# A three-stage tail between attention and gathered rows: two halves of two tiles in place of one tile and three

## What is computed

```
ox_att = _attend_blocks(qx, cat(kx, kc), cat(vx, vc))       # 8 heads, 768 keys
mix_x = _merge(gates, hgrn, conv, ox_att @ w_att_o, w_out)  # (...) @ w_out
x = _layer_norm_2(ALPHA * x + xg1 * mix_x, ln1_g, ln1_b)
t = _modulate(x, xsh2, xsc2)
# _peer(t):
q = (t @ wq).reshape(128, 8, 2, 128)
s1, s2 = q[:, :, 0] @ k1.T, q[:, :, 1] @ k2.T
v1, i1 = lax.top_k(s1, 16); v2, i2 = lax.top_k(s2, 16)
score, ci = lax.top_k(v1[..., :, None] + v2[..., None, :], 16)
expert = i1[ci // 16] * 128 + i2[ci % 16]
g = softmax(score)
act = gelu(einsum('thkd,td->thk', u_tab[expert], t))
out = einsum('thk,thkd->td', g * act, v_tab[expert])
x = _layer_norm_2(ALPHA * x + xg2 * out, ln2_g, ln2_b)
```

## Time and profile before

| | us |
|---|---|
| median of three runs | 4299.42 (4298.96, 4299.42, 4314.07) |
| the profiled execution, its own time | 4277.35 |
| its span in the trace | 4275.5 |
| first indirect load issued | 2539.6 |
| last indirect load issued | 4243.6 |

### The profile page before, as it was taken

How to read it: one execution, slowest core, us unless ns; L and a number is a source line. 1 busy time by engine, 2 the same in 40 slices (tenths; PEclk the granted TensorE clock), 3 DMA queues, 4 the chain that set the end, 5 groups by cost and what they waited for, 6 DMA issues and landing times.

```text
span 4275.5 us, 33127 instructions
## 1 busy us (share of the span) xinstructions
PE 3543.1 (83%) x10814; PEld 1818.0 (43%) x10814; DVE 2175.2 (51%) x4744; ACT 910.9 (21%) x1890; POOL 1332.9 (31%) x1241
## 2 busy tenths in 40 slices
PE   8368998999998989979999974768676878776877
PEld 4244544444454565546544564334232323232323
DVE  0567524421004466756525448864687876433443
ACT  1224412000023124622111312111121212111111
POOL 0200000000000005600001013453777777777775
PEclk9667999999999999979899987889988998899999
DMA  3010021343221212211212356774999999999997
GB/s 149 13 50 1 1 99 66 141 158 136 80 79 47 82 59 74 89 54 60 89 59 79 130 188 217 254 254 173 384 344 351 349 370 364 360 371 372 357 373 284
DMA packets 171914, 765.17 MB, mean 179 GB/s; under 512 B 19256, under 2 KB 19256, under 8 KB 160224
## 3 DMA queue, kind: packets, MB, share of 16 engines
q0 software_dynamic: 157904, 580.06, 36.9%
q1 hardware_dynamic: 13824, 182.97, 11.4%
q10 hardware_dynamic: 16, 0.02, 0.0%
HBM read 744.08 MB, written 18.89 MB: 178 GB/s over the span
## 4 chain that ended last, share of the span: by engine, by line
PE 51%; DVE 15%; issue 9%; POOL 6%; DMA 4%; ACT 3%; another core or an unknown queue 1%; POOLq 0%; DVEq 0%; ACTq 0%
PE ps L252 14%; PE ps L258 12%; POOL arena L2742 6%; PE ps L1406 6%; DVE arena L2772 5%; PE ps L1336 5%; PE ps L2695 5%; DMA arena<-in_pu,arena 3%; PE ps L1712 2%; PE ps L220 2%; DMA arena<-in_pv,arena 1%; PE ps L1699 1%; PE ps L786 1%; PE ps L2320 1%
## 5 line engine op out<-in xcount | busy, mean ns | idle before, releaser
L2695 PE MATMUL ps<-arena 128*128 128x512 f32 x2048 | 1024.1, 649 | 369.7 <-issue 158.6
L2772 DVE CUSTOM_DVE_ANT_0 arena<-arena 128x1024 f32<-128x1024 f32 x512 | 623.5, 1222 | 406.7 <-DMA arena<-in_pu,arena 374.1
L2695 PEld LDWEIGHTS ps<-arena 128*128 128x128 f32 x2048 | 400.3, 205 | 974.2 <-issue 765.6
L252 PE MATMUL ps<-arena 128*128 128x512 f32 (+1 forms) x1768 | 757.7, 589 | 33.2 <-ACT arena L2261 24.4
L2742 POOL DMA_INDIRECT arena<-in_pu,arena x512 | 563.9, 1101 | 406.0 <-issue 95.2
L2742 POOL DMA_INDIRECT arena<-in_pv,arena x512 | 553.7, 1081 | 196.1 <-issue 128.6
L258 PE MATMUL ps<-arena 128*128 128x512 f32 (+2 forms) x1408 | 529.0, 536 | 3.1 <-DVE arena L1253 0.9
L252 PEld LDWEIGHTS ps<-arena 128*128 128x128 f32 x1768 | 338.4, 193 | 438.3 <-issue 433.6
L258 PEld LDWEIGHTS ps<-arena 128*128 128x128 f32 x1408 | 267.2, 190 | 261.1 <-issue 216.9
L263 POOL TENSOR_TENSOR arena<-arena 128x1 f32<-128x1 f32 (+7 forms) x38 | 61.4, 1618 | 997.1 <-DVE arena L630 430.0
L220 PE MATMUL ps<-arena 128*128 128x128 f32 x1046 | 198.8, 327 | 199.0 <-ACT arena L812 49.8
(11 more groups left out here) (342 smaller groups left out, 3332.7 us busy)
## 6 DMA issues: line engine op xcount, KB each, us to landing
arena<-in_w_in SPq DMA_DIRECT2D x27, 2048.0 KB, 8.9
arena<-in_w_ada SPq DMA_DIRECT2D x12, 2048.0 KB, 7.9
arena<-in_w_ff_in SPq DMA_DIRECT2D x8, 2048.0 KB, 12.3
arena<-in_w_ff_out SPq DMA_DIRECT2D x8, 2048.0 KB, 12.4
arena<-in_w_pq SPq DMA_DIRECT2D x8, 2048.0 KB, 8.3
aside<-arena POOLq DMA_DIRECT2D x20, 512.0 KB, 4.7
arena<-in_w_at SPq DMA_DIRECT2D x4, 2048.0 KB, 8.0
arena<-in_w_o SPq DMA_DIRECT2D x4, 2048.0 KB, 8.2
```

The source lines that it names most:

```text
L252: x = t.matmul(PS[:, b, 0:n], hT[:, k, i * 128:(i + 1) * 128], w[:, k, :], start=k == 0, stop=k == nk - 1)
L2695: x = t.matmul(PS[:, b + c, :], DG[n % 4], row(f)[:, 512 * c:512 * c + 512], start=j == 0, stop=j == 127)
L2772: v.tensor_tensor_reduce(row(f), row(f), TT[i], 1.0, 0.0, ALU.mult, ALU.add, DOT[i % 2][:, j:j + 1]).then_inc(*pe.V.step("dot", 128 * i + j))
```

## The change

Part 0 becomes tiles 0 and 1, part 1 tiles 2 and 3. The hooks begin after unit 18 in place of 10 and deal the steps of part 0 alone: no rows are dealt beside the attention (before, `BESIDE` = 30 rows). v rows follow u rows at a fixed distance of 24, where before 64 u rows came first, then one v to four u, then five v to four u. There are 12 places in place of 7 until row 230 (before: 144), and 24 after that (before: 19). Part 1's steps begin at row 8, one in 7 turns (before: row 30, one in 3), and selection gets two steps a turn until row 48 and one after that (before: two until row 128, then two and one by turns). The queries are computed with 256 tokens at a time, in halves of a panel. The buffers are laid out anew to fit.

```diff
-        PARTS = ((0,), (1, 2, 3))
+        PARTS = ((0, 1), (2, 3))
...
-                if p == 0:
-                    b = bank(t, PBANKS[p], tl.A, "q", p, c)
-                    for f in range(4):
+                for half in range(2):
+                    b = bank(t, PBANKS[p], tl.A, "q", p, 2 * c + half)
+                    for f in (2 * half, 2 * half + 1):
                         for k in range(8):
-                            x = t.matmul(PS[:, b, 128 * f:128 * f + 128], w[:, k, 128 * f:128 * f + 128], h[:, k, :], start=k == 0, stop=k == 7)
...
+                            x = t.matmul(PS[:, b, 256 * (f % 2):256 * (f % 2) + 256], w[:, k, 128 * f:128 * f + 128], h[:, k, :], start=k == 0,
+                                         stop=k == 7)
...
+        BEHIND = 24
...
-            goal = 0 if n_ < 64 else (n_ - 64) // 4 if n_ < 128 else 16 + (n_ - 128) * 5 // 4 if n_ < 512 else 512
+            goal = n_ - BEHIND if n_ < 512 else 512
...
-        PLACES = [piece(o_cs + 1024), piece(o_ka + 1024), piece(o_ka + 2048), piece(o_cs), MIXf[:, 0:1024], piece(o_ht + 1024), piece(o_ka)]
+        PLACES = [piece(o) for o in (o_x, o_x + 1024, BASE, BASE + 1024, o_ka, o_ka + 1024, o_ht, o_ht + 1024, o_va, o_va + 1024, o_va + 2048,
+                                     o_qa + 3072)]
...
-        FROM = 144
+        FROM = 230
...
-                        while (min(i, 1), c) not in asked:
+                        while (i // 2, c) not in asked:
...
-        BESIDE = 30
-        HOOK = 10
+        HOOK = 18
...
-                drain(chosen, 2 if r < 128 or turns[0] % 2 else 1)
-                if r >= BESIDE and turns[0] % 3 == 0:
+                drain(chosen, 2 if r < 48 else 1)
+                if r >= 8 and turns[0] % 7 == 0:
                     drain(others, 1)
...
-            left = itertools.islice(work, FIRST + BESIDE)
+            left = itertools.islice(work, FIRST)
...
-        FIRST = 2 * len(pairs(0)) + 2 + 2 + 2 + 2 + 4
+        FIRST = 2 * len(pairs(0)) + 4 + 4 + 2 + 4 + 8
```

More of the change, by code:

```diff
@@ L2358, in tail_scalar @@
             for c in range(4):
-                if p == 0:
-                    a.wait_ge(*tl.P.at("q", p, c))
-                    a.activation(QP0[c], PS[:, held(tl.A, "q", p, c), :], ACT.Copy).then_inc(*tl.A.step("q", p, c))
-                    asked.append((p, c))
-                    yield
-                else:
-                    for f in range(4 * c, 4 * c + 4):
-                        a.wait_ge(*tl.P.at("q", p, f))
-                        a.activation(QP1[f], PS[:, held(tl.A, "q", p, f), 0:384], ACT.Copy).then_inc(*tl.A.step("q", p, f))
-                        if f % 4 == 3:
-                            asked.append((p, c))
-                        yield
+                for half in range(2):
+                    n = 2 * c + half
+                    a.wait_ge(*tl.P.at("q", p, n))
+                    a.activation(QP[p][n], PS[:, held(tl.A, "q", p, n), :], ACT.Copy).then_inc(*tl.A.step("q", p, n))
+                    if half:
+                        asked.append((p, c))
+                    yield
         def tail_other(p, asked, first, each):
@@ L2381, in tail_other @@
                 yield
-            for _ in range(2 * (p == 0) + 2 * len(P)):
+            for _ in range(2 + 2 * len(P)):
                 yield
             for c in range(4):
-                for f in range(4 if p else 1):
-                    if f == (3 if p else 0):
+                for half in range(2):
+                    if half:
                         asked.append((p, c))
@@ L2434, in tail_other_end @@
         def tail_other_end(p, asked):
-            for _ in range(2 * (p == 0) + 2 * len(PARTS[p])):
+            for _ in range(2 + 2 * len(PARTS[p])):
                 yield
             for c in range(4):
-                for f in range(4 if p else 1):
-                    if f == (3 if p else 0):
+                for half in range(2):
+                    if half:
                         asked.append((p, c))
@@ L2474, in first @@
                 if p == 0:
-                    g.wait_ge(*tl.V.at("row0"))
-                for i in P[0:2]:
+                    g.wait_ge(*tl.V.at("rows"))
+                for i in P:
                     load_x(i)
@@ L2590, in select_other @@
                     if h % 2 == 0:
-                        while (min(i, 1), h // 2) not in asked:
+                        while (i // 2, h // 2) not in asked:
                             yield
@@ L2715, in rows_scalar @@
                 yield
-        LATE = [piece(o_x + 1024 * j) for j in range(4)] + [ROW0, GAIN]
-        YY, XHR = MIXf[:, 1024:2048], MIXf[:, 2048:3072]
+        LATE = [piece(o_x + 2048), piece(o_x + 3072), MIXf[:, 2048:3072], MIXf[:, 3072:4096], ROW0, GAIN]
+        YY, XHR = XR[2], XR[3]
         s_late, s_xhr = sem("s_late"), sem("s_xhr")
```

82 lines of the change are left out of this document (35 added, 47 removed).

## The result

| | before | after |
|---|---|---|
| median, us | 4300.04 (4298.96 to 4314.07, 4 runs) | 4343.91 (4329.94 to 4363.1, 4 runs) |
| span of the profiled execution | 4275.5 | 4327.7 (own time 4329.94) |
| first load / 245th load after it / last load | 2539.6 / 3106.4 / 4243.6 | 2643.9 / 3105.8 / 4279.2 |
| from the last load to the end | 31.9 | 48.5 |

The change makes the kernel slower: ratio 1.0086, 95% interval 1.0057 to 1.0116. I had said 0.988, with 4180 to 4312 us as the range.

The account below looks back on a forecast made before the run. Transfers were taken to bound the kernel after 3000 us and to be starved before. Row 221 at 3062, 1130 us for 779 loads and 32 us of end gave span 4224, time 4247 (ratio 0.988), range 4180 to 4312.

Parts of the forecast that it names:

- The attention and part 1: Start up to row 221: first load at 2642 us, 102 us later than before; row 221 done at 3062.
- the slower rival: Late start not made good: PE at lower clock in part 1, time 4370 at mean clock 0.6; chance 0.16.
- One number beside the sum: Start of the loads: some 67 loads of the kernel before are out by 2642 us.
- 245 loads are out: At row 221, 3062 us: POOL has got ahead and filled the new places, 1.67 us per load.
- After 3000 us the transfers bound the kernel, and no engine is full: Late stretch of before: DMA 96% to 97% busy, loads at 1.49 and 1.43 us, DVE and PE not full.
- I take 1.45: Remaining 779 loads: 1.45 us each, between 1.43 without selection and 1.49 with it, 1130 us in all.
- What the change can win is bounded: 250 us, not 461: Starved stretch before 3000 us: its 175 loads would take 250 us at 1.43 us each, not 461.
- The rule I weighed: DVE with two SBUF inputs and POOL share a port pair, so selection taxes loads anywhere: 11 us more.
- I keep 32: From last load to span's end: 32 us as before, though 24 v rows are last, not 18.
- Loads don't get cheaper: After row 221: loads stay at 1.466 us, part 1 costs 25 us more, time 4284; chance 0.19.
- Hides better: PE's bursts vanish behind loads: 779 at 1.42 us, row 221 25 us earlier, time 4198; chance 0.15.
- the signs that I had named: First load near 2642; 245 loads by 3062; then 1.43 to 1.47 us each, DMA 97% busy; part 1 clock over 0.85.

Follow-up runs that it names:

- a_pe: Changed kernel with half of each v row's product on PE left out (256 of 512 columns per product): ratio 0.9983 to the kernel before.
- b_again: The kernel before, unchanged, run once more for its profile on the same chip as other runs: one run, 4304.21 us.
- a_taper: Changed kernel with the distance of v rows behind u rows drawn in from 24 to 18 at the end: ratio 1.0087 to the kernel before.
- a_again: The changed kernel, unaltered, run once more for its profile on another chip: ratio 1.0073 to the kernel before.
- b_sel: Kernel before with the changed kernel's pace of selection (two steps a turn until row 48, then one): ratio 0.9971 to the kernel before.
- b_sel_again: Kernel before with selection at two steps a turn until row 48, then one, repeated on another chip: ratio 1.0001 to the kernel before.

## Why the prediction was wrong

By its own steps, span times of after:

| step | forecast | measured |
|---|---|---|
| PE at the first scores / first load | 2629 / 2642 | 2630.8 / 2643.9 |
| row 40, 60, 96, 116 done | 2737, 2782, 2827, 2880 | 2742, 2775, 2834, 2876 |
| row 166, 221 done | 2943, 3062 | 2955, 3079 |
| 245th load | 3062 | 3106 |
| the 779 loads after it | 1130 | 1173 |
| the end | 32 | 48.5 |
| span | 4224 | 4327.7 |

(A row is done when DVE's product of it, or PE's, has ended; the latest of all rows up to it counts.)

- **The attention and part 1 were right.** Seven marks over 320 us lie within 12 us, the eighth is 17 late, by what no run shows. Granted clock 0.88 there, over the 0.85 I had named: the slower rival (PE at the low clock in part 1, decided at 0.70) did not happen, though the result lies on its side. PE does set most of the pace there: a_pe. One number beside the sum was wrong: of the kernel before 41 loads are out at 2642 us by its trace, not 67.
- **"245 loads are out" at row 221 failed, 27 us.** 230 were out at 3079. I let the twelve new places serve at row 221, but they begin with load 242, and ahead of it stands a narrow place that `FROM` makes: 230 is no multiple of 12, so load 230 gets the place that row 228 holds, and load 231 that of row 229. POOL's timeline of after:

```profile
3083.29 0.94 POOL L2727 DMA_INDIRECT arena<-in_pu,arena  x1 [4.32 <-DVE arena L2757]
3086.45 0.94 POOL L2727 DMA_INDIRECT arena<-in_pv,arena  x1 [2.22 <-PE ps L2680]
```

From there it issues 14 loads in 19.4 us. That another `FROM` would win these 27 us back is read from this timeline; no run tests it.
- **"After 3000 us the transfers bound the kernel, and no engine is full" failed, and with it "I take 1.45", 43 us.** It was 1.506 us a load, above both ends of my bounds (1.43 and 1.49). POOL was full, and the earlier trace rows said so: 461.00 us busy from 3050 to 3650, in the row where I named DVE and PE alone, and 402 gaps of 0.30 us beside it make 582 of 600 us (by its timeline 23 us of waits are left). So the price of a load is what POOL needs for it, and that depends on what DVE does meanwhile. I counted loads as if all were alike, and took their price from the earlier trace rows, where only 72 of the first 245 loads had been v rows. The change fills the starved stretch with v rows and so moves 38 u rows, and two heads of selection, behind it, into the stretch where a product holds POOL. The kernel before does more of its DVE work where POOL waits anyway. "What the change can win is bounded: 250 us, not 461" was true of loads and said nothing of that. That the changed kernel takes 36 us longer than the one before over the same 779 loads is this step again. Alone it would have left 8 of the 51 us of gain; with the 44 us of the late mark and the 17 of the end the sign turns.
- **The rule I weighed was the right one at the wrong place.** I set it against selection's short operations and split the difference; these hold next to nothing (some 7 us of b_again's rest). The u row products, which I didn't look at, do. It stood in the earlier trace rows: 106 loads took 115.63 us there, 16 more than 106 x 0.94, and I read no meaning into it.
- **"I keep 32" failed, 17 us.** I looked at the 24 rows (a_taper: not they) and not at PE's state before them: v rows come one in two loads to the last, PE idles between them, falls to the lower clock (3.75 us a row), is released late by ACT, and stands 18 rows behind. With half of PE's work the end is 33 us, with 12 diagonals 40, against 52 in a_again. How much of it each of these makes stays open, and b_again's end, 40 us against 32 in before, says that the end moves by 8 us by itself.
- **The rivals.** "Loads don't get cheaper" had the right place, but with 1.466 as its worst. "Hides better" was out. Of the signs that I had named, the first load and the clock came as forecast; 245 loads by 3062, 1.43 to 1.47 us a load and DMA 97% busy (it was 95%) did not.

## What to carry to other kernels

When a change fills a starved stretch, ask what the other engines did in it for nothing: that work does not vanish, it moves to where it costs. Count it at the same mark in both kernels (here: DVE's work left at the 245th load), not only the transfers. An engine at 77% busy can be full: add the fixed gap between its instructions to their time before you say that it is not what bounds. And a long wait in the trace, even 20 us with a clear culprit, is proven to cost time only by being removed: here 500 us of them went and the time stayed.

## What the runs showed of the hardware

- An indirect load on POOL that begins within a two-input product on DVE ends 0.82 us behind the product (0.94 us alone); a product that starts within the load lengthens neither the load (0.94 us on average in after) nor itself (1.22 us). A sequence that issues loads just ahead of products might avoid the hold; it was not run.
- Between two indirect loads POOL shows a gap of 0.30 us that nothing in the trace fills (0.30 to 0.32 us before 763 of 779 loads in after). So loads that aren't held come every 1.24 us and no faster.
- ACT was released up to 25 us after the v row that it waited for had ended by PE's record, with PE idle for half of the time meanwhile (16 of the 30 us from 3540 to 3570). A ring of 12 takes most of it away (ACT's idle time 622 to 113 us). Whether the record's end or the update is late stays open.
- The kernel before took 4207 us in one comparison, on a chip of its own, and 4295 to 4300 in the five others. Over 10 us the DMA records show 410 to 416 GB/s at best on the fast chip and on the first; the fast one only holds it longer (two slices of 409 on the page of b_sel, none above 384 in the earlier trace rows). POOL's loads are shorter there as well (825 us for the 779 loads of b_sel, 873 for those of b_sel_again, the same kernel); which of the two comes first stays open.
